# Splitting the last expert quad's output weights, copies, scatter and square sums by halves of the columns

## What is computed

```python
def hier_moe(x, router_grp, router_exp, w1, w3, w2):
    ...
    for e in range(N_EXPERTS):
        hid = jax.nn.silu(xt @ w1[e]) * (xt @ w3[e])
        y = y + combine[:, e:e + 1] * (hid @ w2[e]).astype(jnp.float32)
    ...
hp = hp + hier_moe(...)
hs = hs + hier_moe(...)
y_prompt = rms_norm(hp, ln_f)     # x * rsqrt(mean(x * x) + 1e-6) * ln_f
y_sample = rms_norm(hs, ln_f)
```

## Time and profile before

| what | value |
|---|---|
| median of 3 runs | 887.76 us (885.87 to 892.13) |
| span of the profiled execution (its own time) | 889.2 us |
| TensorE busy, share of the span | 771.0 us, 87% |
| VectorE, ScalarE, GpSimd busy | 43%, 21%, 17% |
| transferred | 220.26 MB, mean 248 GB/s |

### The profile page before, as it was taken

One profiled execution on the slowest core, in us unless ns is written; L12 is line 12 of the kernel. 1 busy time (PEld: TensorE's weight loads), 2 busy tenths in 40 slices (PEclk: granted clock), 3 DMA queues, 4 the chain that ended last, 5 costly groups with the idle time before them and its releaser, 6 DMA issues. The chain is left out here.

```text
span 889.2 us, 20760 instructions
## 1 busy us (share of the span) xinstructions
PE 771.0 (87%) x8681; PEld 454.7 (51%) x8681; DVE 378.6 (43%) x710; ACT 187.0 (21%) x429; POOL 151.4 (17%) x306
## 2 busy tenths in 40 slices
PE   5999899989778979956899887989889997799985
PEld 2445466666566646743566555545454434444411
DVE  3130533239842235466846675723462222422213
ACT  2102122116331111022322321222111110111102
POOL 8400030007040020003323333232000000000000
PEclk9999899998978969968999998989979998999997
DMA  9623141212320212429899999986949999999992
GB/s 320 270 94 119 48 158 48 74 71 85 111 58 20 82 41 45 101 85 362 346 404 368 418 362 419 394 323 221 404 178 428 420 426 421 426 419 426 421 417 77
DMA packets 53047, 220.26 MB, mean 248 GB/s; under 512 B 21871, under 2 KB 23962, under 8 KB 28634
## 3 DMA queue, kind: packets, MB, share of 16 engines
q1 hardware_dynamic: 44976, 183.28, 52.8%
q0 software_dynamic: 7328, 35.48, 10.3%
q10 hardware_dynamic: 650, 0.18, 0.1%
HBM read 211.82 MB, written 7.09 MB: 246 GB/s over the span
## 5 line engine op out<-in xcount | busy, mean ns | idle before, releaser
L230 PE MATMUL bank<-arena 128*128 128x320 f32 x256 | 85.6, 480 | 5.4 <-PEq L112 3.6
L208 POOL DMA_DIRECT2D arena<-in_cv x116 | 59.9, 516 | 112.4 <-PE bank L1831 74.7
L546 PE MATMUL bank<-arena 128*128 128x336 f32 x224 | 71.1, 473 | 4.2 <-DVE arena L712 4.2
L2618 DVE TENSOR_TENSOR arena<-arena,bank 128x512 f32<-128x512 f32 x40 | 27.5, 688 | 109.7 <-PE bank L2399 106.7
L2429 PE MATMUL bank<-arena 128*32 128x512 f32 x512 | 64.6, 607 | 3.7 <-DMA arena<-in_w_exp 2.5
L1524 DVE STREAM_TRANSPOSE arena<-arena 128x2048 f32<-128x2048 f32 x28 | 63.1, 2288 | 5.5 <-DMA arena<-in_ck 4.4
L511 PE MATMUL bank<-arena 128*128 128x512 f32 (+1 forms) x144 | 64.6, 607 | 0.7 <-ACT arena L416 0.7
L230 PEld LDWEIGHTS bank<-arena 128*128 128x128 f32 x256 | 50.2, 207 | 27.3 <-issue 9.9
L546 PEld LDWEIGHTS bank<-arena 128*128 128x128 f32 x224 | 43.8, 200 | 27.3 <-issue 10.0
L1340 ACT ACTIVATE arena<-bank 128x384 f32<-128x384 f32 (+6 forms) x63 | 26.0, 443 | 123.7 <-PE bank L230 46.2
L1831 PE MATMUL bank<-arena 128*16 128x128 f32 x1024 | 35.0, 299 | 17.5 <-issue 9.3
(11 more groups left out here) (491 smaller groups left out, 1115.4 us busy)
## 6 DMA issues: line engine op xcount, KB each, us to landing
arena<-in_w_exp SPq DMA_DIRECT2D x99, 1024.0 KB, 20.2
arena<-in_ck SPq DMA_DIRECT2D x120, 256.0 KB, 6.9
arena<-in_cv POOLq DMA_DIRECT2D x116, 256.0 KB, 9.0
arena<-in_w_gate SPq DMA_DIRECT2D x8, 1024.0 KB, 4.8
arena<-in_w_za SPq DMA_DIRECT2D x7, 1024.0 KB, 6.9
arena<-in_w_zb SPq DMA_DIRECT2D x6, 1024.0 KB, 14.5
arena<-in_w_proj SPq DMA_DIRECT2D x8, 512.0 KB, 10.9
arena<-in_w_out SPq DMA_DIRECT2D x4, 1024.0 KB, 10.8
```

The source lines that it names most:

```text
L208: eng.dma_start(tile[n:P:4, :], src[bass.ds(page, 1)].rearrange("a (p j) n -> (a p) (j n)", j=4))\
L230: mm = nc.tensor.matmul(bank[b][:, 0:TM], w[:, k, a, :], xnT[:, k, NMETA:T], start=(k == 0), stop=(k == KT - 1))
L546: mm = nc.tensor.matmul(bank[j % 2][:, 0:T], w[:, k, (j % 2) * P:(j % 2 + 1) * P], xnT[:, k, :], start=(k == 0), stop=(k == KT - 1))
```

## The change

- The eight half transfers. The last quad's `w2` is no longer loaded by four transfers of 1 MB, but by eight of 512 KB: first the left 512 output columns of each of the four experts, then the right 512 of each. In each of 128 partitions that is two runs of 2 KB where it was one of 8 KB. The right halves have semaphores of their own.
- TensorE in the last quad: the left half's matmuls, then the turning of the combine weights, then the scatter of pieces 0 and 2 (the left columns), then the right half's matmuls (now waiting for `last_full`), then pieces 1, 3 and 4.
- ScalarE in the last quad: copy of the left half, of `gT`, the root's table, then copy of the right half. The square sums go by pieces (five of 512 columns), and the root takes the sum with scale 1/1024 and bias epsilon.
- VectorE: the adds go in the order 0, 2, 1, 3, 4; `mean` adds the two piece sums of a tile; for the sampled tile it is gone, and the root reads the small matmul's result.

```diff
-                for q, part, j in ring[FIRST:]:
+                for q, part, j in ring[FIRST:-QE]:
...
+                for half in range(2):
+                    for j in range(QE):
+                        if half == 0:
+                            sp.wait_ge(*freed(LQ, 2, j))
+                        cols = lambda a: a.rearrange("p (f n) -> p f n", f=2)[:, :, half * HALF:(half + 1) * HALF]
+                        sp.dma_start(cols(place[load_slot(LQ, 2, j)]), cols(A["w_exp"][QE * LQ + j, 2]))\
+                            .then_inc(S(f"last_full{j}") if half else full[load_slot(LQ, 2, j)], 16)
...
+                def scatter_last(places):
+
+                    pe.wait_ge(S("gT_sb"), LQ + 1)
+                    for n in places:
+                        pe.wait_ge(S("yg_sb"), 2 * LQ + (1 if n < 2 else 2))
+                        if n >= 2:
+                            pe.wait_ge(S("hacc"), NHT * LQ + n - 1)
+                        spread(LAST_ORDER[n], bank[6 + n % 2]).then_inc(S("ys_ps"), 1)
...
                     for half in range(2):
+                        if q == LQ and half:
+                            turn_weights(q)
+                            scatter_last((0, 1))
...
+                                if q == LQ and half and f == 0:
+                                    pe.wait_ge(S(f"last_full{j}"), 16)
...
-                scatter(NQD - 1)
-                pe.wait_ge(S("ss3"), NT)
+                scatter_last((2, 3, 4))
+                pe.wait_ge(S("ss3"), NHT)
...
+                    outputs_half(0)
+                    if q == LQ:
+                        turned_weights()
+                        nc.scalar.activation(rt_x, ones[:, 0:1], ACT.Sqrt)
+                    outputs_half(1)
...
+                def root(i, sums):
+                    nc.scalar.activation(rt[:, i:i + 1], sums, ACT.Sqrt, bias=eps[:, 0:1], scale=1.0 / DM)\
+                        .then_inc(S("rt3"), 1)
...
+                for p in range(3):
+                    square(p)
+                for i in range(NT - 1):
+                    square(3 + i)
                     act.wait_ge(S("ms3"), i + 1)
...
+                act.wait_ge(S("pair_f"), 1)
+                root(NT - 1, bank[5][:, 0:1])
...
+                for p in range(4):
+                    accumulate_last(p)
                 mean(0)
+                accumulate_last(4)
                 result(0)
-                accumulate(NQD - 1, (2,))
                 mean(1)
                 result(1)
-                mean(2)
                 result(2)
```

More of the change, by code:

```diff
@@ L2345, in build @@
         ybank = (0, 1, 2, 3, 6)
+        LQ = NQD - 1
+        assert ring[-QE:] == [(LQ, 2, j) for j in range(QE)]
+        LAST_ORDER = (0, 2, 1, 3, 4)
+        ssh = small[:, 4 * NT + 1:4 * NT + 1 + NHT]
+        eps = small[:, 4 * NT + 1 + NHT:4 * NT + 2 + NHT]
+        assert 4 * NT + 2 + NHT <= 32
         with nc.Block("moe") as block:
@@ L2442, in scatter, with turn_weights @@
                         spread(n, bank[6 + n % 2]).then_inc(S("ys_ps"), 1)
+                def scatter_last(places):
[5 more added lines that the diff above has]
+                        spread(LAST_ORDER[n], bank[6 + n % 2]).then_inc(S("ys_ps"), 1)
+                def turn_weights(q):
+                    pe.wait_ge(S("gw_ready"), q + 1)
+                    if q:
+                        pe.wait_ge(S("hacc"), NHT * q)
+                    for i in range(NT):
+                        mm = nc.tensor.transpose(bank[6][:, i * P:(i + 1) * P], gselw[:, q % 2, i, :], ident)
+                    mm.then_inc(S("gT_ps"), 1)
                 def outputs(q):
@@ L2464, in outputs @@
                         mm.then_inc(S("y_ps"), 1)
[L2465 to L2471, removed]
+                    if q < LQ:
+                        turn_weights(q)
                 def overflow(p):
@@ L2522, in _ @@
                     outputs(q)
-                scatter(NQD - 1)
-                pe.wait_ge(S("ss3"), NT)
-                nc.tensor.matmul(bank[5][:, 0:1], pair, ss[:, NT - 1:NT], start=True, stop=True)\
+                scatter_last((2, 3, 4))
+                pe.wait_ge(S("ss3"), NHT)
+                nc.tensor.matmul(bank[5][:, 0:1], pair, ssh[:, NHT - 1:NHT], start=True, stop=True)\
                     .then_inc(S("pair_f"), 1)
@@ L2577, in _, with outputs_half @@
                         act.wait_ge(S("ys_ps"), NHT * q)
[L2578 to L2586, removed]
+                    def outputs_half(half):
+                        act.wait_ge(S("y_ps"), 2 * q + half + 1)
+                        nc.scalar.activation(ygh(half), bank[4 + half][:, :], ACT.Copy).then_inc(S("yg_sb"), 1)
@@ new lines, in turned_weights @@
+                    def turned_weights():
+                        act.wait_ge(S("gT_ps"), q + 1)
+                        nc.scalar.activation(gT, bank[6][:, 0:NT * P].rearrange("p (i t) -> p i t", i=NT), ACT.Copy)\
+                            .then_inc(S("gT_sb"), 1)
+                    outputs_half(0)
[3 more added lines that the diff above has]
+                    outputs_half(1)
+                    if q < LQ:
+                        turned_weights()
@@ new lines, in square @@
+                def square(p):
+                    n = LAST_ORDER[p]
+                    act.wait_ge(S("hacc"), NHT * LQ + p + 1)
+                    nc.scalar.activation(jk[:, n, :], h2[:, n, :], ACT.Square,
+                                         accum_out=ssh[:, n:n + 1]).then_inc(S("ss3"), 1)
+                def root(i, sums):
+                    nc.scalar.activation(rt[:, i:i + 1], sums, ACT.Sqrt, bias=eps[:, 0:1], scale=1.0 / DM)\
+                        .then_inc(S("rt3"), 1)
+                act.wait_ge(S("eps_set"), 1)
@@ L2587, in _ @@
+                for p in range(3):
+                    square(p)
+                for i in range(NT - 1):
+                    square(3 + i)
                     act.wait_ge(S("ms3"), i + 1)
[L2588 removed]
+                    root(i, ms[:, i:i + 1])
+                act.wait_ge(S("pair_f"), 1)
+                root(NT - 1, bank[5][:, 0:1])
             @block.vector
@@ L2706, in _, with accumulate_last @@
                         ch.at, ch.n = n_pass * per + before, 0
+                def accumulate_last(p):
+                    dve.wait_ge(S("ys_ps"), NHT * LQ + p + 1)
+                    h = h2[:, LAST_ORDER[p], :]
+                    nc.vector.tensor_tensor(h, h, bank[6 + p % 2][:, :], add).then_inc(S("hacc"), 1)
                 def mean(i):
[L2708 to L2714, removed]
+                    dve.wait_ge(S("ss3"), 3 + i)
+                    ch(TT(ms[:, i:i + 1], ssh[:, 2 * i:2 * i + 1], ssh[:, 2 * i + 1:2 * i + 2], add))
                     dve.sem_inc(S("ms3"), 1)
```

4 lines of the change are left out of this document (3 added, 1 removed).

## The result

The changed kernel takes 884.12 us (median of 20 runs, 877.47 to 889.56) for 887.95 (20 runs, 880.34 to 893.42). The ratio is 0.9948, with a 95% interval of 0.9924 to 0.9972: 0.5% faster, which is 4.6 us of 887.95, and at least 2.5. (The two medians themselves lie 3.8 us apart.) The forecast was 884.4.

What follows compares the result with a forecast made beforehand. The prediction took the queue of the last expert weights and the tail behind them to bound the end. From the profiled 889.2 it took 2.0 and 2.75 for 884.4 us, own range 882.5 to 886, wider range 881.0 to 888.0.

Steps and rivals of the forecast that it cites:

- What bounds the end: End of kernel: the weights' queue sets when the last quad may be multiplied; 4.19 MB of `w2` and 20 us of tail are open.
- The transfers: Last `w2` loads: 2 KB runs at 388 GB/s for 425 cost 0.9 us more, last expert ready at 870.2 for 869.3.
- TensorE up to the right half: Last quad: left half done at 867.2, clock rises about 868.7, right half runs 870.4 to 872.3, for 874.3 before.
- The first term: TensorE's last quad: the last `w2` matmul ends 2.0 us earlier than in the profiled execution before.
- The tail: After the last `w2` matmul: last product ends 8.7 us later and not 11.45, 2.75 us won.
- The sum: Whole kernel: 889.2 - 2.0 - 2.75 = 884.4 us, from the profiled execution.
- both ways lead to 884.4: Whole kernel: subtracting from the profiled execution, or 3.3 us from the 887.76 median, gives the same 884.4.
- if the right half starts on a scatter's end: Sign of being wrong, in TensorE's last quad: it was to show that the early pieces hold the right half.
- rival 1: TensorE's last quad: clock stays at half until 872.1, early pieces hold the right half, 1.7 us later, 886.1; chance 0.20.
- 2: Last transfers: norm's rows and 2 KB runs meet, landing at 871.1 to 871.6, total 885.6; chance 0.10.
- 3: SyncE's issues fall behind: with two holds the last half lands 7.4 us after forecast, 891.8; chance 0.07.
- 4: Last `w2` loads: small transfers don't overlap, eight take 20.8 us in place of 10.8, 894.4; chance 0.03.

Runs made afterwards that it cites:

- e1: Kernel before with only the eight half transfers, each expert waiting for both halves: fourth expert's matmuls start 0.35 us later, its eight steps take 3.59 us for 4.99.
- e5: Changed kernel with the norm's weights issued only after the last right half landed: right half takes 1.92 us for 2.31.
- e2: Changed kernel with the old tail (square sums by tile, mean and epsilon on VectorE): last product ends 9.84 us after the last `w2` matmul, for 8.73.
- e3: Kernel before with the changed tail alone, pieces in natural order: last product ends 11.23 us after the last `w2` matmul, for 11.45.
- e4: Kernel before with five filler identity matmuls in TensorE's idle times of the last quad: the eight steps take 3.62 us for 4.99.
- e7: Changed kernel with all of `w2` laid out by column halves, runs of 4 KB for 2 KB: right half takes 1.92 us for 2.31.
- e6: Changed kernel with pieces 0 and 2 scattered behind the right half: last product ends 10.0 us after the last `w2` matmul, for 8.73.
- e8: Changed kernel with norm weights issued later, 4 KB runs, combine weights turned earlier, root's table loaded earlier, earlier mean: ratio to the kernel before 0.9948.
- the combined version: Changed kernel with later norm weights, 4 KB runs, earlier turning, table load and mean; timed twice: ratios to the kernel before 0.9948 and 0.9912.

## Why the prediction was right, point by point

- **What bounds the end**: right. The queue of weights, the last landing and the tail are where the gain was made; from L on 5.3 us of it by the two profiles.
- **The transfers**: the mechanism right, the sizes off. The term "0.9 us more" was mis-sized. The halves cost 0.35 us at the fourth expert's start in e1 and 0.5 in the changed kernel (L + 11.32 for 10.82). The stretch at 414 us gave 388 GB/s; here the same runs went at 402. The loss beside the norm's weights, "0.95", which I left in, is there: e5 shows 1.0 us at the last landing, to be had by issuing them later. No hold of SyncE mattered: its last weights were issued by 860.2, which is 858.9 in the time of before, 6 us ahead of the 865.0 that I had worked out for the pitch of 2.18.
- **TensorE up to the right half**: the order of events right, the clock wrong in this execution. I left the fall at 865.27 in and let it rise at 868.7; it never fell. My value for the start, 870.4 in the time of before (L + 11.9), was L + 10.9 (and 11.3 for the last expert). The first term was 2.0 and measured 2.6 against the profile of before (15.81 to 13.23), but 1.2 against a kernel before whose clock stays full (10.82 + 3.6 = 14.4 from L). E1 against the changed kernel gives 1.5 for the order, less 0.35 for the halves.
- **The tail**: E + 8.7 forecast, 8.73 measured; E + 11.45 before. The steps fit too: first late add at E + 1.87 for 1.91, first product at E + 4.61 for 4.66. One detail was wrong and stayed hidden: the squares of pieces 0 and 2 are not done in the wait but after the right half's copy, 1.3 us that fit under the adds. And the tail's gain is no sum of parts, as e2 and e3 show.
- **The sum**: from L on, by the profiles, 2.6 + 2.7 = 5.3 with a fallen clock before, 1.2 + 2.7 = 3.9 without. Of the four profiles of the old order (before, e1, e3, and e4 with its fillers) the clock fell in two. The measured 4.6 (2.5 to 6.7) cannot part the 5.3 from the 3.9. My sum has an error: 889.2 - 2.0 - 2.75 starts from a span, while the metric is the time, 1.6 us longer. From the profile it should have come to about 886.0, the upper end of my own range. The second way started from the median time and took off 3.3 us, since I held the profiled execution to be 1.4 us above the median and put this down to its clock. It was about 3.1 above, and since single executions reach L at different times for other reasons (857.3 to 860.1 in nine profiles), the excess of one says nothing of its last quad. So "both ways lead to 884.4" was a coincidence. The terms of the mechanism stand; that the total came out at 884.4 for 884.12 is luck.
- **My signs of being wrong**: one of them, "if the right half starts on a scatter's end", came true. The right half starts the moment TensorE is free of pieces 0 and 2. The sign was badly chosen: my own sum had that start too (870.4, weights at 870.2), and what tells rival 1 from the forecast is the clock of that stretch, 1.00. The others did not come: the wait for weights ends at 871.10, which is 869.8 in the time of before, the last weights are issued at 859.03 (857.7), and there is one table load.
- **Rivals**: 1 (the pieces hold the right half at half clock) was not met in five profiles of this order (the changed kernel twice, e2, e5, e7). It is not refuted: in e6 the clock fell in this stretch, and with the pieces ahead E would have been some 1.0 us later (the estimate at e6), which is less than the 1.7 I had given it. 2 did not occur at its size: the fourth expert starts at L + 11.32, where 871.1 would be L + 12.6. Its cause, the norm's rows beside runs of 2 KB, is real and is in the measured 11.32. 3 did not occur. 4 is refuted by the rate of 402 GB/s. The Trainium skill's advice of 1 MiB or more ("DMA: Bandwidth & Descriptors", Measured) does not carry over to transfers that stand in a full queue: what counted here was the run in a partition, 402, 420 and 423 GB/s at 2, 4 and 8 KB, the first two with transfers of 512 KB. The page's figures are for transfers issued by GpSimd, and so is the formula in the prediction, which stands under Anatomy of one DMA and not under Measured; the transfers here are issued by SyncE.

## What to carry to other kernels

Where the last transfer sets the end, split what waits for it along the output, not the sum, so that one half's whole way behind it (copies, scatter, adds) runs while the other half is still coming; then look at what the early work holds up, since the two ends should meet. Lay the split data out so that each part is one run, and keep transfers that are needed only later out of the last one's company. And measure such steps from a landmark inside the profile: here two profiles of one kernel agree to 0.01 us from L on, while the totals of one kernel lie 5 to 13 us apart. Compare spans with spans and times with times. What such a landmark leaves out, a change ahead of it, only the timed runs can show.

## What the runs showed of the hardware

- The full DMA engines moved 423 GB/s with runs of 8 KB, 420 with 4 KB, 402 with 2 KB in the same stage of three versions of the kernel.
- SyncE's row of the half transfers in the changed kernel, and the landing row behind it:

```profile
L2374 SPq DMA_DIRECT2D arena<-in_w_exp x8: 607/2721/9237, 833.4 to 859.0; - x8
...
DMA to landing us min/median/max: 10.9/15.8/28.2
```

  The shortest time from issue to landing fell from 23.7 us to 10.9 with 2 KB runs, and is 17.6 in e8 with 4 KB runs. So with shorter runs fewer bytes stood ahead of a transfer in the queue; what the queue counts is not shown. One issue held SyncE for 9.2 us. It cost nothing here: behind the weights SyncE had only the norm's rows to issue, which came in time.
- Each transfer lands in sixteen parts, and the trace holds the time of each. In the changed kernel fourteen parts of the last transfer are in by L + 9.47, the last two come at L + 11.10 and 11.28. In e5, without the norm's reads beside it, the fourteenth comes at L + 9.10, the last two at 10.25 and 10.29. So two of the sixteen set the end in both, and the norm's reads delay mostly these two.
- In these rows a pass of a float32 matmul over 512 columns starts 0.43 us after the one before it at the full clock and 0.85 at half; the same eight steps took 3.6 or 5.0 to 5.3 us depending on where the fall lay. Between L and the tail it fell in three of twelve profiles: before (at L + 6.8), e6 (L + 6.6) and e3 (L + 11.6). Only the changed and the combined version were profiled twice, and in those four it stayed full; why it fell in the three is not shown.
